# The odd mixer of each chunk of 128 tokens laid beside the other chunk's expert rows, and 512 gathers in one series

## The reference, cut to what matters

```
for layer in range(2):
    xn = rmsnorm(h, norm_mix[layer])
    h = h + (attn_retention_mixer if layer == 0 else short_conv_mixer)(xn, ...)
    h = h + peer(rmsnorm(h, norm_ffn[layer]), w_q[layer], sub_keys[layer], u[layer], v[layer])
return rmsnorm(h, final_norm)

def short_conv_mixer(xn, w_in, conv_w, w_out):      # the "odd" mixer
    bg, cg, hx = split(xn @ w_in, 3)                 # w_in is 1024 x 3072
    y = causal_conv_width_3(cg * hx, conv_w)         # a channel at a time, over tokens
    return (bg * y) @ w_out

def peer(xn, w_q, sub_keys, u, v):                   # 8 heads, 16 experts each of 16384
    q = (xn @ w_q).reshape(tokens, 8, 2, 128)
    sc = q . sub_keys                                # two lists of 128 scores a head
    top 16 of each list, top 16 of their 256 sums -> eidx, gate = softmax
    hid = gelu(xn . u[eidx])                         # row product
    return sum over 128 (head, k): gate * hid * v[eidx]
```

## Time and profile before

| | us |
|---|---|
| median of 3 runs | 2401.3 |
| range | 2395.9 to 2408.8 |
| profiled execution, its own time | 2407.2 |
| its span | 2405.4 |
| granted TensorE clock, mean | 0.95 of full |

### The profile page before, as it was taken

The page is one execution under the profiler, slowest core; times in us unless marked ns, Lnnn a source line. Parts: engine busy times, 40 slices in busy tenths (PEclk is TensorE's granted clock), DMA queues, the critical chain, the costliest instruction groups (busy, mean ns, idle before and its releaser), DMA issues.

```text
span 2405.4 us, 18927 instructions
## 1 busy us (share of the span) xinstructions
PE 1948.4 (81%) x5904; PEld 958.4 (40%) x5904; DVE 1240.6 (52%) x3256; ACT 500.3 (21%) x1260; POOL 632.8 (26%) x594
## 2 busy tenths in 40 slices
PE   7999896987859868888777777799688887777776
PEld 4445563333224444444232223286444442232222
DVE  1315244111012347776777776403577677777764
ACT  1212330111101112222222222200122222222221
POOL 1102000111000013433444444200134344444442
PEclk9999897999979989999999999999799999999999
DMA  7532405899864278999999999734789999999996
GB/s 231 164 114 77 164 14 207 364 419 418 354 220 140 88 262 346 416 417 410 422 410 422 421 421 419 313 120 139 269 337 405 393 387 421 417 422 422 421 422 264
DMA packets 159079, 750.99 MB, mean 312 GB/s; under 512 B 16561, under 2 KB 45793, under 8 KB 80641
## 3 DMA queue, kind: packets, MB, share of 16 engines
q0 software_dynamic: 78928, 542.37, 54.9%
q1 hardware_dynamic: 77744, 198.39, 22.5%
q10 hardware_dynamic: 2304, 8.99, 1.1%
HBM read 751.79 MB, written 10.49 MB: 317 GB/s over the span
## 4 chain that ended last, share of the span: by engine, by line
DMA 27%; PE 18%; DVE 12%; issue 9%; POOL 4%; ACT 1%; POOLq 0%; DVEq 0%; ACTq 0%
DMA arena<-in_c_rows_dram,arena 26%; DVE arena L1922 5%; PE banks L1769 4%; POOL arena L1976 4%; PE banks L295 4%; PE banks L2061 4%; PE banks L1908 2%; PE banks L401 2%; DVE arena L1856 1%; DVE arena L1860 1%; DVE arena L1818 1%; PE banks L1782 1%; PE banks L323 1%; DVE arena L1865 1%; DVE arena L1821 1%
## 5 line engine op out<-in xcount | busy, mean ns | idle before, releaser
L1908 PE MATMUL banks<-arena 128*128 128x512 f32 x2048 | 955.3, 614 | 273.2 <-ACT arena L1965 264.3
L1976 POOL DMA_INDIRECT arena<-in_c_rows_dram,arena x512 | 553.7, 1081 | 838.7 <-PE banks L1908 527.7
L1922 DVE CUSTOM_DVE_ANT_0 arena<-arena,xn 128x1024 f32<-128x1024 f32 x512 | 625.3, 1223 | 272.4 <-DMA arena<-in_c_rows_dram,arena 271.2
L1908 PEld LDWEIGHTS banks<-arena 128*128 128x128 f32 x2048 | 380.4, 194 | 838.9 <-ACT arena L1965 430.9
L295 PE MATMUL banks<-ring,hT 128*128 128x512 f32 (+1 forms) x736 | 318.5, 590 | 7.7 <-DMA ring<-in_w_in_dram 4.5
L1965 ACT ACTIVATE arena<-ident,small 128x128 f32<-128x128 f32 x512 | 177.6, 394 | 501.8 <-DVE small L1929 499.4
L295 PEld LDWEIGHTS banks<-ring,hT 128*128 128x128 f32 x736 | 138.4, 194 | 168.1 <-issue 161.7
L329 ACT COPY arena<-banks 128x512 f32<-128x512 f32 (+4 forms) x175 | 85.5, 508 | 534.0 <-PE banks L323 150.3
L355 POOL TENSOR_TENSOR small<-small 128x1 f32<-128x1 f32 (+4 forms) x24 | 34.1, 1425 | 553.7 <-DVE small L351 553.7
L334 DVE COPY arena<-banks 128x512 f32<-128x512 f32 (+1 forms) x51 | 34.8, 682 | 223.8 <-PE banks L1118 84.4
L1958 ACT ACTIVATE small<-small 128x2 f32<-128x2 f32 x256 | 52.0, 203 | 373.9 <-DVE small L1922 373.9
(11 more groups left out here) (257 smaller groups left out, 1486.7 us busy)
## 6 DMA issues: line engine op xcount, KB each, us to landing
ring<-in_c_experts_dram SPq DMA_DIRECT2D x48, 1024.0 KB, 25.1
arena<-in_c_experts_dram SPq DMA_DIRECT2D x48, 1024.0 KB, 24.9
ring<-in_w_in_dram SPq DMA_DIRECT2D x30, 1024.0 KB, 5.2
ring<-in_peer_w_q_dram SPq DMA_DIRECT2D x16, 1024.0 KB, 5.7
ring<-in_even_w_in_dram SPq DMA_DIRECT2D x14, 1024.0 KB, 5.1
ring<-in_odd_w_in_dram SPq DMA_DIRECT2D x12, 1024.0 KB, 5.8
arena<-in_c_rows_dram,arena POOLq DMA_INDIRECT x512, 13.3
ring<-in_w_out_dram SPq DMA_DIRECT2D x4, 1024.0 KB, 6.3
```

The costliest lines, as they stand in the source:

```text
L1908: r = e.matmul(banks[:, bank_of[("acc", L, c, hf)], :], diag[:, m % NDIAG, :], rows[:, m % NB, D + hf * 512:D + (hf + 1) * 512], start=fir ...
L1922: e.tensor_tensor_reduce(u, u, xn[:, c, :], 1.0, 0.0, ALU.mult, ALU.add, hid3[:, c, h, k:k + 1]).then_inc(ve.sem, ve.up(("u", p)))
L1976: e.indirect_dma_start(rows[:, b, :], None, table_uv, bass.IndirectOffsetOnAxis(ap=eix[:, c, 16 * h + k:16 * h + k + 1], axis=0)).then_inc ...
```

## The change

Positions 0 to 511 are now one series on every engine, and POOL asks for all 512 rows in a row. The odd mixer and layer 1's scores are cut into steps that a table, `beside`, puts at positions: `pe_beside`, `act_beside` and `dve_beside` do what stands at p. With `base` = 128 (c + 1), chunk c's norm `mix1` stands at base + 4, its in-projection at base + 9 to 56 (one matmul of 128x512 a position; tokens on partitions), turned tiles, convolution of eight parts and gate product in between, the output product at base + 60 to 75, the norm `ffn21` at base + 76, and the scores of layer 1's heads 0 and 1 at base + 81 and 91. Heads 2 to 7 follow at 16 positions' distance in the segment after. So chunk 0's mixer runs beside chunk 1's layer-0 rows, chunk 1's mixer beside chunk 0's layer-1 rows.

Other parts:
- Every weight of the odd mixer and of layer 1's `w_q` is loaded once for each chunk, and the in-projection's tiles are 4 x 512 instead of 8 x 256 wide.
- In positions 128 to 383, every fourth row's v half (`on_dve`) is weighed and added to `x` by DVE; PE and ACT do nothing for it.
- The mixer's tiles have places of their own in `arena`.
- POOL makes the root of a norm behind the ask of p + 5 (`AHEAD`).
- Chunk 0's final norm stands at 388; each chunk has its own output transfer.

The diff, cut to its core:

```diff
+AHEAD = 5
...
+        yT = ub.rearrange("p (k t) -> p k t", k=8)
+        bgb = place(512)
+        uT = place(8 * 130).rearrange("p (k t) -> p k t", k=8)
...
-        def scores_at(p):
-
-            r = p % (2 * SEG)
-            return r // 16 + 2 if r % 16 == 4 and r // 16 < 6 else None
-
-        def choice_at(p):
-
-            r = p % (2 * SEG)
-            if r == 0:
-                return 0, 1, 5
-            if r % 16 == 8 and r // 16 + 2 < 16:
-                return (r // 16 + 2) // 8, (r // 16 + 2) % 8, 3
-            return None
-
-        def sync_peer(e, layer):
-            w = kview(a["peer_w_q_2"][layer])
+        LAST = len(SLOTS)
+        w_q = [kview(a["peer_w_q_2"][L]) for L in range(2)]
+        w_odd, w_odd_out = kview(a["odd_w_in_2"][0]), kview(a["odd_w_out_2"][0])
+
+        def on_dve(m):
...
+            return m // SEG in (1, 2) and m % 4 == 3
...
+        OB = (("cg", 0), ("hx", 0), ("cg", 1), ("hx", 1), ("bg", 0), ("bg", 1))
+        OCOL = {"bg": 0, "cg": 1024, "hx": 2048}
+        beside = {}
+        choices_at = {0: (0, 0, 1, 5)}
+
+        def put(p, *what):
+            beside.setdefault(p, []).append(what)
+
+        def norm_steps(p, n, c):
+            put(p, "square", n, c)
+            put(p + 1, "mean", n, c)
+            put(p + 2, "normed", n, c)
+
+        def head_steps(p, c, h):
+            for i in range(8):
+                put(p + i, "q", c, h, i)
+            put(p + 9, "sc", c, h)
...
+        for h in range(2, 8):
+            put(16 * (h - 2) + 4, "scores", h)
+        for j in range(2, 16):
+            choices_at[16 * (j - 2) + 8] = (0, j // 8, j % 8, 3)
+        put(12, "gain", "ffn21", "ffn20")
+        put(SEG + 2, "keys")
+        for c in range(2):
+            base = SEG * (c + 1)
+            norm_steps(base + 4, "mix1", c)
+            put(base + 5, "edge", c)
+            put(base + 7, "turn", "mix1", c)
+            for j in range(6):
+                for k in range(8):
+                    put(base + 9 + 8 * j + k, "in", c, j, k)
+            for hf, at_u, at_b in ((0, 26, 50), (1, 42, 58)):
+                put(base + at_u, "turn_u", c, hf)
+                for k in range(4):
+                    put(base + at_u + 2 + k, "conv", c, 4 * hf + k)
+                put(base + at_b, "turn_b", c, hf)
+            for hf in range(2):
+                for k in range(8):
+                    put(base + 60 + 8 * hf + k, "out", c, hf, k)
+            norm_steps(base + 76, "ffn21", c)
+            put(base + 79, "turn", "ffn21", c)
             for h in range(8):
-                load(e, ("wq", layer, h), w[:, :, 256 * h:256 * (h + 1)], 8)
+                head_steps(base + (81, 91)[h] if h < 2 else base + SEG + 16 * (h - 2) - 2, c, h)
+                choices_at[base + (100, 112)[h] if h < 2 else base + SEG + 16 * (h - 2) + 8] = (1, c, h, 3)
+        put(2 * SEG + 20, "gain", "fin", "mix1")
+        norm_steps(3 * SEG + 4, "fin", 0)
...
+                    if what[0] == "in" and what[3] % 4 == 0:
+                        _, c, j, k = what
+                        col = OCOL[OB[j][0]] + 512 * OB[j][1]
+                        load(e, ("odd", c, j, k), w_odd[:, k:k + 4, col:col + 512], 4)
+                    if what[0] == "out" and what[3] % 4 == 0:
+                        _, c, hf, k = what
+                        load(e, ("oddout", c, hf, k), w_odd_out[:, k:k + 4, 512 * hf:512 * hf + 512], 4)
+                    if what[0] == "q" and what[3] == 0:
+                        _, c, h, _ = what
+                        load(e, ("wq", 1, c, h), w_q[1][:, :, 256 * h:256 * (h + 1)], 8)
...
+            if kind == "in":
+                _, c, j, k = what
+                name, w = ("O", c, j), ("odd", c, j, k - k % 4)
+                if k == 0:
+                    _, before = rings.take(name, hold=True)
+                    if before is not None:
+                        e.wait_ge(*emptied[before])
+                    await_hT(e, "mix1", c)
+                wt = tile(e, w, 4)
+                r = e.matmul(banks[:, bank_of[name], :], hT[:, k, c * P:(c + 1) * P], wt[:, k % 4, :],
...
+            if kind == "q":
+                _, c, h, i = what
+                name = ("q", 1, c, h)
+                if i == 0:
+                    _, before = rings.take(name, hold=True)
+                    if before is not None:
+                        e.wait_ge(*emptied[before])
+                    if h == 0:
+                        await_hT(e, "ffn21", c)
+                wt = tile(e, ("wq", 1, c, h), 8)
+                f = i // 4
+                for k in (2 * (i % 4), 2 * (i % 4) + 1):
+                    r = e.matmul(banks[:, bank_of[name], f * P:(f + 1) * P], wt[:, k, f * P:(f + 1) * P],
+                                 hT[:, k, c * P:(c + 1) * P], start=(k == 0), stop=(k == 7))
...
+            if kind == "conv":
+                _, c, k = what
+                g = fetched("conv")
+                e.wait_ge(g.sem, g.at("all"))
+                e.wait_ge(ac.sem, ac.at(("uT", c, k // 4)))
+                chain(e, ve)
+                e.tensor_scalar(yT[:, k, :], uT[:, k, 0:128], cw[:, k:k + 1], None, ALU.mult).then_inc(ve.sem, ve.up())
+                for i in (1, 2):
+                    e.wait_ge(ve.sem, ve.n)
+                    e.scalar_tensor_tensor(yT[:, k, :], uT[:, k, i:i + 128], cw[:, 8 * i + k:8 * i + k + 1],
+                                           yT[:, k, :], ALU.mult, ALU.add).then_inc(ve.sem, ve.up())
...
-        def pe_position(e, p, lo, hi):
-            h = scores_at(p)
-            if h is not None and p < hi:
-                pe_score(e, p // (2 * SEG), h, (0, 1))
-            if p % 2 and p - 3 >= lo:
+        def pe_position(e, p):
+            for what in beside.get(p, ()):
+                pe_beside(e, what)
+            if p % 2 and p >= 3:
                 for m in (p - 3, p - 2):
-                    if m < hi:
+                    if m < LAST and not on_dve(m):
                         pe_value(e, m)
+
+        def last_on_pe(m):
+            end = m - m % SEG + SEG - 1
+            return end - 1 if on_dve(end) else end
 
         def pe_value(e, m):
             L, c, h, k = SLOTS[m]
-            first, last = (h, k) == (0, 0), (h, k) == (7, 15)
+            first, last = (h, k) == (0, 0), m == last_on_pe(m)
...
+                if on_dve(p - 1):
+                    e.wait_ge(ve.sem, ve.n)
+                    e.scalar_tensor_tensor(x[:, c, :], rows[:, (p - 1) % NB, D:2 * D], hid3[:, c, h, k + 1:k + 2],
+                                           x[:, c, :], ALU.mult, ALU.add).then_inc(ve.sem, ve.up(("v", p - 1)))
+            if p % SEG == 3 and p > 3:
                 dve_collect(e, p - 4)
-            new = choice_at(p) if p < hi else None
-            if new is not None:
-                L = p // (2 * SEG)
-                choices[:] = [dve_choose(e, L, new[0], new[1]), new[2]]
+            for what in beside.get(p, ()):
+                dve_beside(e, what)
+            if p in choices_at:
+                L, c, h, rate = choices_at[p]
+                for _ in choices[0] if choices else ():
...
+            for p in range(LAST):
+                if p + AHEAD < LAST:
+                    pool_ask(e, p + AHEAD)
+                for what in beside.get(p, ()):
+                    if what[0] == "mean":
+                        pool_norm(e, what[1], what[2])
```

More of the change, by code:

```diff
@@ new lines, in act_beside @@
+        def act_beside(e, what):
+            kind = what[0]
+            if kind == "scores":
+                act_score(e, 0, what[1], (0, 1))
+            if kind == "gain":
+                e.wait_ge(ve.sem, ve.at(("xn", what[2], 1)))
+                gain_fetch(e, what[1])
+            if kind == "keys":
+                e.wait_ge(pe.sem, pe.at(("sc", 0, 7, (0, 1))))
+                g = fetched("kt1")
+                e.dma_start(kt, a["c_keys"][1]).then_inc(g.sem, g.up("all", by=16))
+            if kind == "square":
+                _, n, c = what
+                e.wait_ge(ve.sem, ve.at({"mix1": ("x", "peer", 0, c), "ffn21": ("oddres", c, 1),
+                                         "fin": ("x", "peer", 1, c)}[n]))
+                act_square(e, n, c)
+            if kind == "turn":
+                act_turned_chunk(e, what[1], what[2])
+            if kind == "in" and what[3] == 7:
+                _, c, j, _ = what
+                kind_, hf = OB[j]
+                if kind_ != "hx":
+                    dst = bgb if kind_ == "bg" else ub[:, 512 * hf:512 * hf + 512]
+                    act_unload(e, ("O", c, j), dst, banks[:, bank_of[("O", c, j)], :])
+            if kind == "turn_u":
+                _, c, hf = what
+                e.wait_ge(ve.sem, ve.at(("edge", c)))
+                act_unload(e, ("uT", c, hf), uT[:, 4 * hf:4 * hf + 4, 2:130], turned(("uT", c, hf), P, 4))
+            if kind == "q" and what[3] == 7:
+                _, c, h, _ = what
+                e.wait_ge(pe.sem, pe.at(head_before(c, h)))
```

(8 more changed lines are left out.)

329 lines of the change are left out of this document (167 added, 162 removed).

## The result

The changed kernel takes 2342.8 us (median of 4 runs, 2340.2 to 2342.9), the kernel before 2401.5. The ratio is 0.9751, with a 95% interval of 0.9724 to 0.9778: 58.7 us less, where 55 were forecast. Its profiled execution has a span of 2341.0 us, 64.4 less than before.

The account below looks back on a forecast made before the run. DMA engines were taken to bound the expert stage. Terms -189.0 (gap, slow start), -2 (end), +126 (loads), +5 (keys, gains), +5 (waits) gave -55 us: 2401.3 to 2346, own range 2335 to 2361, wider range 2314 to 2384.

Parts of the forecast that it names:

- The bound: Expert stage of both layers: the 16 DMA engines set the pace, while every other engine has idle time.
- The pace: Gathered rows in the expert stage: 2.51 us for each set of 128 rows of 8 KB.
- What goes, 189.0: Gap between the layers' rows, 154.1 us, and layer 1's slow first half, 34.9 us, both vanish.
- The load price, 42 x 3.0 = 126: Rows 128 to 383: 42 additional 1 MB weight loads between gathers cost 3.0 us each on DMA.
- Five for waits: Mixer steps beside rows: DVE, ACT and PE run in order and wait for each other, adding 5 us.
- The engines' cover: Rows 128 to 383: added work hides under DMA; DVE 296 of 375 us, PE 257 of 375 and 282 of 393.
- SP holds up nobody: SP's load queue: six slots fetch some 60 us ahead of loads landing 10.4 us after issue; only loads wait.
- The cushion of 5.9 us: Nine row buffers: of each 8.2 us PE stop for scores, 5.9 us go unseen by DMA.
- Loads at their bytes: Rival: loads cost only their bytes, 2.49 us each, and extra waits vanish; 2318 us, 2310 to 2335; chance 0.17.
- Bunched waits: Rival: in-order waits of neighbouring mixer steps exceed the cushion, up to 45 us; 2361 to 2390; chance 0.16 up to 2388.
- Asks held by additions: Rival: 64 value additions on DVE hold up POOL's asks, up to 83 us, 2429; chance of slower 0.06.
- Late numbers: Rival: layer 1's expert numbers come late, leaving a hole at row 256; 2370 and up; chance counted with another rival.

Follow-up runs that it names:

- All on PE: Changed kernel with no value row on DVE, all 512 going through PE as before the change: 2341.2 us.
- half on DVE: Changed kernel with every second instead of every fourth value row of positions 128 to 383 on DVE: 2343.5 us.
- bursts: Changed kernel with each in-projection and output block of the mixer in one piece, eight matmuls at the last of its eight positions: 2343.6 us.
- half loads: Changed kernel fetching only half the bytes of the odd mixer's and layer 1's w_q weight loads, same packet sizes, computing other numbers: 2276.3 us.
- packed loads: Changed kernel with odd mixer and layer 1 w_q weights laid out in HBM tile by tile, each load 128 packets of 8 KB: 2327.1 us.
- Eight buffers: Changed kernel with eight row buffers instead of nine, and the root of a norm behind the ask of p + 4: 2345.5 us.

## Why the prediction was right

- **The bound.** Right. I took DMA as the bound of the rows beside the mixer and gave the stretches 375, 393 and 321 us; they took 376.3, 394.5 and 321.2. All on PE, half on DVE and bursts move other engines' work and leave these lengths alone; half loads and packed loads move bytes and packets and change them.
- **The pace.** The 320.2 us of rows 128 to 255 before, and the same 320.2 from the first to the last row product of the last stretch, hold 127 paces and not 128, so a row takes 2.52 us where I had 2.51. It changes no bound and takes 1.4 us out of what goes.
- **What goes, 189.0.** Of the 154.1 of the seam all is gone (2.5 us between the products). The slow first half of layer 1 went with it: its rows need the quiet 2.5 plus loads. At 2.52 it was 33.4 rather than 34.9, and 187.6 in all.
- **The load price, 42 x 3.0 = 126.** Right in its cause, a little high in size: the balance of the two stretches is 2.84, so 119. The size came from the block of layer 0 and the packet time; the bytes alone (2.49) would have been wrong by more. The Trainium skill's overhead of three beats per packet (DMA: Bandwidth & Descriptors, Why small descriptors are slow) would by my estimate let packing save some 5.5 us (2.3 on the 26 loads in 2 KB packets, 3.3 on the 16 in 1 KB ones); packing saved 12.0 us in the two stretches, so the rows were right to follow. Packed, the loads cost 2.54, their packet time.
- **Five for waits.** Not seen: with a price of 2.84, no more than the packet times give, nothing is left over, and all-on-PE and bursts changed the waits without moving the time. In-order waits exist, but DMA keeps its line of asks through them. The additions, 136 by my terms, were 123: 13 too high. The tail gave 0.7 (17.7 us from the last product to the end, 18.4 before) where I took 2.
- **The sum.** The span fell by 64.4, of which 2 lie before the expert stage, and I had forecast 55 of the span; the medians fell by 58.7. That 2342.8 lies so close to 2346 is in part luck: the profiled execution of the kernel before, from which I worked, was 5.7 us above its median, and that makes up for more than half of the miss in the terms.
- **The engines' cover.** DVE 296 of 375 was 300 of 376. PE 257 was 280 and 282 was 298: the granted clock in these stretches was 0.88 and 0.89 where 0.98 stood before, which I had not forecast. It was covered all the same.
- **SP holds up nobody.** Wrong, harmlessly: in the line beside gathers a tile takes 12 us in 2 KB packets and 21 in 1 KB ones, and PE stood 33.7 us for four tiles of w_q. I had sized a load by the 10.4 us it took in layer 0, where loads were few. Packed loads show this wait gone.
- **The cushion of 5.9 us.** Wrong as a property of nine buffers. Eight buffers should then have shown each burst of layer 0; rows 16 to 96 took 2.1 us more in all. Where there are bursts the edge lies between eight and seven, in the quiet stretch between seven and six. What the 11.4 us were (10.5 at a pace of 2.52) that five bursts cost in layer 1 before, with nine buffers and no loads beside them, I didn't test; beside loads (layer 0, before and after) such bursts leave no mark, 215.4 being 201.7 and five loads at 2.7.
- **The rivals.** Loads at their bytes: refuted by packing. Bunched waits: bursts made them worse for 1 us. Asks held by additions: the asks are longer by 0.2 us, the path isn't. Late numbers: not late, with 33 us in hand.

## What to carry to other kernels

If a gather stage is bound by DMA and the work between two such stages is not, lay that work beside the gathers even at the price of loading its weights twice: 42 loads at 2.84 us each were paid out of a hole of 154 us and a slow start of 33. Price the moved loads by the time of their packets, and lay weights out in HBM so that a load is one long packet a partition: that alone gave another 13 to 16 us. Before moving vector or matrix work to and fro for balance, look whether either engine ends the wait: here the same length came out with PE at 247 or 308 us.

## What the runs showed of the hardware

- A 1 MB load beside saturated gathers of 8 KB rows cost 2.84 us in packets of 1 and 2 KB and 2.54 in packets of 8 KB; packet times were 2.97 (rows 256 to 383) and 2.52.
- While both had work, SP's queue and the gathers' queue moved about as many packets each (1339 and 1336 in 30 us, 2430 and 2484 in 50 us), though a gather's packet held 8 KB and SP's 2 or 1. SP's loads so got 88 GB/s with 2 KB packets and 49 with 1 KB ones, of 411 to 413 in all.
- With work taken off PE its granted clock was lower, and its busy time fell by less than the work removed: 0.98 and 0.96 in the two stretches with all values on PE, 0.88 and 0.89 with a quarter on DVE, 0.83 and 0.84 with half. The 32 rows moved in the first of them would be 59 us at 3.70 us for two; PE's busy time fell by 28, from 308 to 280. All three stood beside the same DMA load. Each is a mean between the two levels, 2.4 and 1.2 GHz. I did not test what makes the clock fall; PE stood idle more.
- POOL's asks took 1.07 us in the mean without additions on DVE in the stretch and 1.27 with 32 of them. The Trainium skill (SBUF — State Buffer, Who interferes with whom) has a DVE instruction with two SBUF inputs block a GpSimd read of SBUF; the longer asks agree with it. That 64 additions gave 1.25 and not more is not explained by it.
